# A hybrid mLSTM and pooling layer on one core: modulation with its weights stationary, ten tiles of x scaled on GpSimd and turned by plain transposes, gate columns in two passes

## The reference

```python
def _adaln(cvec, w, b):
    m = jax.nn.silu(cvec) @ w + b          # (1024) @ (1024, 3072)
    return jnp.split(m, 3, axis=-1)        # shift, scale, gate
...
shift, scale, gate = mod_x                 # from c
shift_c, scale_c, gate_c = mod_c           # from c_ctx, the same ada_w
parts_x = _split_proj((_rmsnorm(x, norm_w) * (1 + scale) + shift) @ in_w)
parts_c = _split_proj((_rmsnorm(xc, norm_w) * (1 + scale_c) + shift_c) @ in_w)
...
pre = parts['gates'] + gate_b              # 16 columns of in_w: log_i and log_f, 2 directions, 4 heads
log_f = jax.nn.log_sigmoid(pre[:, 1])
```

## Time and profile before

| | us |
|---|---|
| median of 3 runs | 2520.41 |
| lowest and highest | 2520.32, 2527.89 |
| the profiled execution, its own time | 2523.78 |
| its span in the trace | 2521.8 |
| PE busy | 2401.8 (95% of the span) |
| DVE busy | 1202.1 (48%) |
| ACT busy | 819.6 (33%) |

### The profile page before, as it was taken

The page is one execution under the profiler, slowest core; times in us unless marked ns, Lnnn a source line. Parts: engine busy times, 40 slices in busy tenths (PEclk is TensorE's granted clock), DMA queues, the critical chain, the costliest instruction groups (busy, mean ns, idle before and its releaser), DMA issues. The chain is left out here.

```text
span 2521.8 us, 35743 instructions
## 1 busy us (share of the span) xinstructions
PE 2401.8 (95%) x12923; PEld 2039.3 (81%) x12923; DVE 1202.1 (48%) x2323; ACT 819.6 (33%) x1694; POOL 317.7 (13%) x323
## 2 busy tenths in 40 slices
PE   7899999999999999999999989999999689999998
PEld 5667888888888877888888878788888579797978
DVE  2612212222222225566666757676766355646564
ACT  2521111111111113343434434344444335353532
POOL 1011000000000002121112211222121112121210
PEclk9999999999999999999999999999999899999999
DMA  8337555434533437787677797867777545666563
GB/s 250 119 78 246 127 91 130 125 93 120 135 92 119 128 85 235 212 207 222 198 231 238 216 317 224 232 179 234 212 221 230 179 153 193 204 201 200 193 209 109
DMA packets 464343, 453.15 MB, mean 180 GB/s; under 512 B 23997, under 2 KB 405589, under 8 KB 462637
## 3 DMA queue, kind: packets, MB, share of 16 engines
q1 hardware_dynamic: 423484, 386.16, 50.3%
q10 hardware_dynamic: 33296, 33.56, 7.2%
q0 software_dynamic: 7392, 31.15, 3.2%
HBM read 310.73 MB, written 140.05 MB: 179 GB/s over the span
## 5 line engine op out<-in xcount | busy, mean ns | idle before, releaser
L1200 PE MATMUL bank<-xlate,wh 128*128 128x512 f32 x2048 | 673.8, 403 | 10.8 <-DVE v_t L1334 5.0
L1200 PEld LDWEIGHTS bank<-xlate,wh 128*128 128x128 f32 x2048 | 375.0, 190 | 81.5 <-DVE v_t L1334 5.4
L1200 PE MATMUL bank<-xlate,wl 128*128 128x512 f32 x1024 | 411.3, 402 | 0.0
L627 PE MATMUL bank<-xearly,wh 128*128 128x512 f32 (+1 forms) x1280 | 367.0, 372 | 0.0
L627 PE MATMUL bank<-xlate,wh 128*128 128x512 f32 x1024 | 321.8, 396 | 0.0
L627 PEld LDWEIGHTS bank<-xearly,wh 128*128 128x128 f32 x1280 | 228.5, 188 | 39.0
L627 PE MATMUL bank<-xearly,wl 128*128 128x512 f32 (+1 forms) x640 | 236.9, 370 | 0.0
L627 PEld LDWEIGHTS bank<-xlate,wh 128*128 128x128 f32 x1024 | 191.0, 189 | 39.2
L1200 PEld LDWEIGHTS bank<-xlate,wl 128*128 128x128 f32 x1024 | 194.5, 190 | 34.1
L627 PE MATMUL bank<-xlate,wl 128*128 128x512 f32 x512 | 201.4, 393 | 0.0
L833 DVE SCALAR_TENSOR_TENSOR qks<-bank,qks 128x512 fp32r<-128x512 f32 (+1 forms) x72 | 47.5, 660 | 301.8 <-ACT qks L703 301.7
(11 more groups left out here) (259 smaller groups left out, 4516.1 us busy)
## 6 DMA issues: line engine op xcount, KB each, us to landing
v_t<-vk_d SPq DMA_DIRECT2D x144, 384.0 KB, 4.3
qk_d<-qks SPq DMA_DIRECT2D x64, 512.0 KB, 2.7
q_t<-qk_d SPq DMA_DIRECT2D x128, 256.0 KB, 5.4
wraw<-in_in_w_dram ACTq DMA_DIRECT2D x31, 1024.0 KB, 12.7
wraw<-in_in_w_dram SPq DMA_DIRECT2D x32, 512.0 KB, 9.2
vk_d<-vs SPq DMA_DIRECT2D x64, 256.0 KB, 2.8
k_t<-qk_d SPq DMA_DIRECT2D x64, 256.0 KB, 6.5
wraw<-in_branch_m_w_dram SPq DMA_DIRECT2D x32, 512.0 KB, 3.8
```

The source lines that it names most:

```text
L627: mm = pe.matmul(bank[m % 4][:, 0:w], a[:, u % 2, k, :], xn(b, k, t0, w), start=(k == 0 and n == 0), stop=(k == KT - 1 and n == 2))
L1200: mm = pe.matmul(bank[m % 2][:, :], a[:, u % 2, k, :], xlate[part][:, k, tq * TQ:(tq + 1) * TQ], start=(k == 0 and n == 0), stop=(k == KT ...
```

## The change

1. **Modulation.** The slice of `ada_w` becomes stationary (128x128) and `sc` (2 columns) moves, so that columns come out directly; `copy_row`, `turn_row` and `mrow` go. The 24 slices and their order stay.
2. **Loads.** All loads of x and ctx move from POOL's queue to SP's, into one order with the slices: tile n behind slice n+4; later `rows_in` of a group ahead of that group's two slices. XS goes from 9 to 10.
3. **x.** The squares of groups 0 to 2 (NSC = 3, ten tiles) run ahead of the x stage; POOL multiplies these ten tiles by 1/rms in place, and PE turns them by plain transposes. Groups 3 and 4 keep the diagonal; their squares run in groups 2 and 3, at j = 2 to 5, `scales` and the four diagonals behind j = 6. PE may be four banks ahead of ACT, not two.
4. **Gates.** The weights' high and low parts lie side by side as 32 columns; x-high meets all 32, x-low the first 16: two matmuls for each k, not three. 32 rows are stored, eight loads bring them back, and DVE adds the halves in head 0 (`g_sum`). `grow` becomes a ring of three. The split of the gate weights moves from the end of the first block to ahead of the x stage.

```diff
-            XS, YS, GS = 9, 2, 8
-            WS1 = 3
+            XS, YS, WS1 = 10, 2, 3
+            NSC, QT1 = 3, TQ // P
+            XBANKS = [bank[n] for n in (0, 2, 3, 6)]
...
+                def weights_in(f):
+                    if f >= WS1:
+                        sp.wait_ge(aw_used, f - WS1 + 1)
+                    sp.dma_start(aw[:, f % WS1], ada_v[:, :, f * P:(f + 1) * P]).then_inc(aw_loaded[f % WS1], 16)
+                def rows_in(n):
+                    g, r = tiles[n]
+                    if n >= XS:
+                        sp.wait_ge(x_turned, KT * (tiles[n - XS][0] + 1))
+                    t0 = r * P + (0 if g == 0 else groups[g][1] - CTX)
+                    sp.dma_start(xt[:, n % XS, :], groups[g][3][t0:t0 + P, :]).then_inc(x_loaded[n % XS], 16)
...
+                for f in range(NEARLY):
+                    weights_in(f)
+                    if 4 <= f < 4 + XS:
+                        rows_in(f - 4)
+                sp.wait_ge(gz, 1)
+                sp.dma_start(gbias[0:NGATE, :], gate_b[0].rearrange("(a b) -> a b", b=1)).then_inc(g_loaded, 16)
+                sp.dma_start(wg[:, :, :], in_v[:, :, GATE0:GATE0 + NGATE]).then_inc(g_loaded, 16)
+                for g in range(1, len(groups)):
+                    for n in range(XS, NCH):
+                        if tiles[n - XS][0] == g - 1:
+                            rows_in(n)
+                    for f in later(g):
+                        weights_in(f)
...
+                for n in range(first[NSC]):
+                    pool.wait_ge(norm_dve, GSTEP * (tiles[n][0] + 1))
+                    pool.tensor_scalar(xt[:, n % XS, :], xt[:, n % XS, :], rstd[:, n:n + 1], None, ALU.mult).then_inc(x_scaled, 1)
...
-                    if n >= 2:
-                        pe.wait_ge(row_made, n - 1)
+                    dst = mod[:, f] if f < NEARLY else mod_gate[:, f - NEARLY]
                     for k in range(KT):
-                        mm = pe.matmul(bank[6 + n % 2][0:2, 0:AS], sc[:, k, :], aw[:, n % WS1, k, :],
-                                       start=(k == 0), stop=(k == KT - 1))
+                        mm = pe.matmul(dst, aw[:, f % WS1, k, :], sc[:, k, :], start=(k == 0), stop=(k == KT - 1))
                     mm.then_inc(aw_used, 1)
...
-                        if m >= 2:
-                            pe.wait_ge(y_made, m - 1)
+                        if m >= 4:
+                            pe.wait_ge(y_made, m - 3)
...
+                            if g < NSC:
+                                mm = pe.transpose(dst, src, ident[:, :])
+                            else:
+                                mm = pe.matmul(dst, src, diag[:, n - first[NSC], :], start=True, stop=True)
...
-                        if g >= 1 and g + 1 < len(groups):
-                            if j < TQ // P:
-                                squares(first[g + 1] + j)
-                            elif j == TQ // P:
+                        if NSC - 1 <= g and g + 1 < len(groups):
+                            if 2 <= j < 2 + QT1:
+                                squares(first[g + 1] + j - 2)
+                            elif j == 2 + QT1:
                                 root(g + 1)
...
                 for d in range(2):
-                    for k, dst in ((0, gi[d]), (1, gf[d])):
+                    for k, dst in ((0, gi[d]), (1, gf[d]), (NGATE // HEADS, gm[d]), (NGATE // HEADS + 1, gb[d])):
...
                     for k in range(KT):
-                        for n3, (a, b) in enumerate(((wgh, 0), (wgh, 1), (wgl, 0))):
-                            mm = pe.matmul(bank[6 + n % 2][0:NGATE, 0:w], a[:, k, :], xn(b, k, t0, w),
-                                           start=(k == 0 and n3 == 0), stop=(k == KT - 1 and n3 == 2))
+                        pe.matmul(bank[6 + n % 2][0:2 * NGATE, 0:w], wgs[:, k, :], xn(0, k, t0, w),
+                                  start=(k == 0), stop=False)
+                        mm = pe.matmul(bank[6 + n % 2][0:NGATE, 0:w], wgs[:, k, 0:NGATE], xn(1, k, t0, w),
+                                       start=False, stop=(k == KT - 1))
...
-                    if n >= 1:
-                        act.wait_ge(g_stored, 16 * n)
+                    if n >= 3:
+                        act.wait_ge(g_stored[n % 3], 16 * (n // 3))
...
+                    dve.wait_ge(g_back, 128)
+                    for d in range(2):
+                        dve.tensor_tensor(gi[d][:, :], gi[d][:, :], gm[d][:, :], ALU.add).then_inc(g_sum, 1)
+                        dve.tensor_tensor(gf[d][:, :], gf[d][:, :], gb[d][:, :], ALU.add).then_inc(g_sum, 1)
```

More of the change, by code:

```diff
@@ L192, in _ @@
                                         base=0, pattern=[[-1, P]], channel_multiplier=1).then_inc(ident_made, 1)
[L193 to L201, removed]
+                pool.memset(gbias[:, :], 0.0).then_inc(gz, 1)
+                for n in range(first[NSC]):
+                    pool.wait_ge(norm_dve, GSTEP * (tiles[n][0] + 1))
+                    pool.tensor_scalar(xt[:, n % XS, :], xt[:, n % XS, :], rstd[:, n:n + 1], None, ALU.mult).then_inc(x_scaled, 1)
             @block.tensor
@@ L267, in root @@
                     act.activation(rt[:, a:b], ms[:, a:b], ACT.Sqrt).then_inc(rooted, 1)
-                for g in range(2):
+                for g in range(NSC):
                     squares(*range(first[g], first[g + 1]))
                     root(g)
+                act.wait_ge(g_loaded, 32)
+                act.activation(wgs[:, :, 0:NGATE], wg[:, :, :], ACT.Copy).then_inc(g_hi, 1)
                 for g, (w, t0, kind, _) in enumerate(groups):
@@ L318, in scales @@
                     dve.tensor_tensor(rstd[:, a:b], rstd[:, a:b], newton[:, 2, a:b], ALU.mult).then_inc(norm_dve, 1)
[L319 to L342, removed]
+                for g in range(NSC):
+                    scales(g)
+                dve.wait_ge(g_hi, 1)
+                dve.tensor_tensor(wgs[:, :, NGATE:2 * NGATE], wg[:, :, :], f32(wgs[:, :, 0:NGATE]), ALU.subtract).then_inc(g_lo, 1)
+                dve.wait_ge(aw_used, NEARLY)
                 for a in range(2):
@@ L355, in _ @@
                     for j in range(KT):
-                        if g >= 1 and g + 1 < len(groups) and j == TQ // P + 1:
-                            scales(g + 1)
                         m = KT * g + j
@@ L364, in _ @@
                                           ALU.subtract).then_inc(y_split, 1)
[L365 to L372, removed]
+                        if NSC - 1 <= g and g + 1 < len(groups) and j == 2 + QT1:
+                            scales(g + 1)
+                            dve.wait_ge(norm_dve, GSTEP * (g + 2))
+                            for n in range(first[g + 1], first[g + 2]):
+                                dve.tensor_scalar(diag[:, n - first[NSC], :], ident[:, :], rstd[:, n:n + 1], None,
+                                                  ALU.mult).then_inc(diag_made, 1)
+                dve.wait_ge(aw_used, NF)
+                dve.tensor_tensor(mgate[:, :], mod_gate[:, 0:KT, 0],
                                   vcol[:, VR["ada"] + 2 * KT:VR["ada"] + 3 * KT], ALU.add).then_inc(mod_dve, 1)
@@ L547, in _ @@
                     pool.wait_ge(g_row, n + 1)
-                    pool.dma_start(gates_d[:, t0:t0 + w], grow[:, 0:w]).then_inc(g_stored, 16)
-                pool.wait_ge(g_stored, 16 * len(gpieces))
+                    pool.dma_start(gates_d[:, t0:t0 + w], grow[:, n % 3, 0:w]).then_inc(g_stored[n % 3], 16)
+                for n in range(3):
+                    pool.wait_ge(g_stored[n], 16 * len(range(n, len(gpieces), 3)))
                 for d in range(2):
-                    for k, dst in ((0, gi[d]), (1, gf[d])):
+                    for k, dst in ((0, gi[d]), (1, gf[d]), (NGATE // HEADS, gm[d]), (NGATE // HEADS + 1, gb[d])):
                         r = 2 * HEADS * d + HEADS * k
```

83 lines of the change are left out of this document (30 added, 53 removed).

## The result

The kernel after takes 2533.2 us (median of 7 runs, 2531.28 to 2545.47) against 2520.41 of before beside it; the ratio is 1.005, 95% interval 1.0032 to 1.0068. In a second series it took 2530.91 (10 runs) against 2522.63, 1.0035 (1.002 to 1.0049). It is slower, by some 8 to 13 us, where I had forecast 3.5 us faster. The forecast of 2516.9 was wrong; the time lies in the range, between the two rivals in which the clock stays low (2539 throughout, 2527 in the opening only).

A forecast was written before the change was run, and what follows sets the result against it. Loads were taken to bound the opening, with PE close behind and busy 95% of the whole span. Terms +0.5 + 2.2 - 8.0 + 1.8 = -3.5 took 2520.4 to 2516.9 us; the 8-in-10 range was 2506 to 2540.

The forecast's parts named there:

- the two rivals in which the clock stays low: PE's clock low through opening and turned groups, 2539 us, chance 0.27; or low only in the opening, 2527, chance 0.14.
- Opening, forecast +0.5: Up to the first y: slices at 1.9 us at full clock, loads the bound, first y at 54.3, +0.5 us.
- the rival: Clock low through opening and turned groups: slices 3.5 us, first y 64.2, total 2539 us; chance 0.27.
- x stage, forecast +2.2: First y to block end: -3.0 group 1, +4.5 group 2, +1.0 group 3, -0.3 tail, giving +2.2 us.
- Step 12 comes 1.6 late, the second slice costs 0.5: 10.7: x stage, group 1: slice 16 waits behind two x tiles; the group takes 10.7 us, a gain of 3.0.
- 4.5 late: x stage, group 2: slice 18 waits behind four x tiles, step 20 ready 4.5 us after ACT wants it.
- The diagonals of groups 3 and 4, forecast +1.0 each: x stage: diagonals made at the previous group's end, so PE turns nothing ahead; +1.0 for group 3, 0.7 for group 4.
- my upper bound of 2.40: Scaling one x tile on POOL takes between about 1.05 and 2.40 us; four stay covered, no loss taken for DVE.
- Gates, forecast -8.0: Second block's gate pieces: 80 matmuls, not 120, a PE wait of 4.1 us and 2.4 for low clock; -8.0 us.
- Recurrence, forecast +1.8: Head 0: ACT's chain waits for DVE's adds until 162.6, lengthening PE's later wait; +1.8 us.

The follow-up runs named there:

- e3: Kernel after, with SP asking for a group's two slices ahead of its x tiles: 2516.71 us, 0.9974 of before.
- e4: Kernel before with the modulation's weights made stationary as its only change: 2528.56 us, 1.0024 of before.
- e1: Kernel after with 128 moving columns in place of 2 in each modulation matmul: 2520.13 us, 0.9987 of before.
- e9: e7 with the first ten tiles of x scaled on ACT instead of POOL: 2510.03 us, 0.9954 of before.
- e7: Kernel after with both 128 moving columns in the modulation and slices ahead of x tiles on SP: 2508.96 us, 0.9945 of before.
- e11: e7 with squares, root and diagonals two steps earlier in groups 2 and 3: 2507.45 us, 0.9941 of before.
- e8: Kernel after once more, unchanged: 2530.91 us, 1.0035 of before.
- e2: Kernel before with the gate columns in two passes as its only change: 2518.03 us, 0.9982 of before.
- e10: e2 with x tiles asked for on SP, interleaved with the slices (slices first), instead of on POOL: 2516.5 us, 0.9986 of before.

## Why the prediction was wrong, step by step

**Opening, forecast +0.5, measured +8.7.** This is the first step that failed: "The diagonal matmuls load 128 columns for each of 16 records in 2.05 us, so I take 1.9 us a slice at the full clock, no change". The 1.9 was right for the full clock (1.84 in e3 and e4). That PE would have that clock was taken over from the diagonals and the old opening, where 128 columns move; with two columns behind each load it stays low as long as nothing else runs. e4 shows it by this part alone and e1 takes it back by columns alone. I had the rival's bounds from rows (3.5 a slice, first y at 64.2; measured 3.41 and 62.56) and gave it 0.27, because full-length matmuls bring the clock up in the rows. They were not what would run. (The rival's price adds 10.4 us to a forecast that already holds 0.5 of them; 9.9 would have been right.)

**x stage, forecast +2.2, measured +14.0.** This is the larger miss, 11.8 us against the opening's 8.2, and the second step that failed, by its terms for groups 1 and 2: "Step 12 comes 1.6 late, the second slice costs 0.5: 10.7" and "**4.5 late**". From its first y to the next group's, group 1 took 15.3 us (10.7 forecast) and group 2 took 25.1 (18.2, and 1.0 for the diagonals behind it). The places of the waits were right, the sizes not. Slice 18 landed 10.4 after the last turn of group 1 (10.0 forecast), but ACT waited 8.09 and not 4.5, and it waited before that, too, for slice 16 and for slices at 3.41. The order of SP explains nearly all of it: e3 takes 12.2 back. The rival put its 11.5 of this stage on the clock and so had the times nearly right (15.5 and 21.5 for the two groups; measured 15.3 and, without the wait for the diagonals, 21.7), but that was half a cause. With the waits gone the clock came up in e3 by itself, and with wide slices and the waits kept e1's stage gained only 2.3, so idling and low clock are one loss here, not two to be added. The Trainium skill (TensorE: Matmul & The Clock Gate, Part 4: PE-mode transpose) has it that the full clock doesn't engage for transposes, which don't count as PE being busy. The traces differ, and they decide: e3's transposes ran at the high clock between two-column slices (1.07 for eight), and in e9 the clock came up from 0.50 to 1.00 behind 24 transposes with nothing else on PE. So the rule gave no extra time here.

**The diagonals of groups 3 and 4, forecast +1.0 each.** PE waited 3.44 and 3.40, and in e7, where less else was late, 7.47 and 3.40; e11 won 6.5 us of stage there by making them earlier. Undersized.

**POOL's scalings.** One takes 2.84 us, above my upper bound of 2.40:

```profile
L213 POOL TENSOR_SCALAR xt<-xt,rstd 128x1024 f32<-128x1024 f32 x10 | 28.3, 2842 | 34.2 <-DVE rstd L321 34.2
```

I took no loss for DVE. In the kernel after it is nearly nothing (one cast of 0.98 at 63.16 before POOL was done at 64.0), only because the first y was already late. In e7, where it isn't, group 0's casts and subtractions run 0.6 to 0.8 longer each time that POOL holds them; e9 removed that, but ACT's queue gave it back.

**Gates, forecast -8.0, measured -7.8.** Right, with its steps: a wait of 4.97 on ACT's copy, and the low clock for 5.9 us behind it.

**Recurrence, forecast +1.8.** The chain starts 1.66 later as forecast, behind the adds. PE's wait ends only 0.3 later: what the chain lost at its start it mostly regained before PE needed it; where, isn't known.

**The sum.** 8.7 + 14.0 - 7.8 is +14.9 at head 0 (164.05 less 149.06 is 15.0). The medians moved by 12.8 and 8.3. Between head 0 and the end stand two unexplained things. One is scatter, shown by e8. The other may be systematic: the median less the trace's start of head 0 is 2371 to 2378 for before, e2 and e10, and 2364 to 2372 for the others. The queue of the x tiles is not the reason (e10). The traces say where to look: in all fourteen it is 795.3 to 797.0 us from head 0 to the start of block 3's projections, and 546.5 to 549.5 from their end to the kernel's, but the projections themselves span 1012.6 to 1032.0. What lengthens them stays open, and with it why the gates' 9.2 us bring only 4.4 alone.

## What to carry to other kernels

When operands change places, count the moving columns and not only the loads: a stream that is nearly all weight loads ran here at the pace of the low clock for 50 us, and junk columns made it faster. Where a queue's order is rewritten, look at what PE wants first behind each wait: slices behind two and four tiles of x cost 12 us, low clock included, and swapping two loops returned them. Price a helper engine by what it does to its neighbours, and again after every mend, since a lateness elsewhere can hide it.

## What the runs showed of the hardware that was not expected

- Matmuls of 128x128 stationary by 2 moving fp32 columns took 0.214 us a record for as long as 52 us without the clock rising (after, e4), and 0.115 (1.84 for 16) when diagonals or transposes stood between them (e3, e4). With 128 moving columns the record takes 0.128 (2.05 for 16).
- Behind 24 plain transposes with nothing else on PE the granted clock rose from 0.50 to 1.00 (e9, 58.90 to 64.98).
- The clock column reads 1.00 over the opening although the pace is that of the low clock (after, e3, e4).
- Scaling a 128x1024 fp32 tile by a column takes 2.84 us on POOL (after) and 1.05 on ACT (8.40 for eight, e9), and POOL's stretches DVE's 256-column cast from 0.29 to as much as 1.09 and its subtraction from 0.43 to 1.22 (e7).
- Two executions of one program differed by 10.4 us in block 3, with the first block the same to 0.4 us.
